# Splitting the last 512 columns of a residual stage, and the first pair of an activation, in a two-block transformer kernel

## The reference, cut to what matters

```python
for i in range(DEPTH_2):
    mod = (c_act @ mod_w[i] + mod_b[i]).reshape(B, 6, D)[:, :, None, :]
    hin = x * (1.0 + mod[:, 1]) + mod[:, 0]
    y = mla_mixer(hin, ...) if i == 0 else moba_mixer(hin, ...)      # ends in  merge_heads(o) @ w_o
    x = layer_norm(DEEPNORM_ALPHA * x + mod[:, 2] * y, ln_g[i, 0], ln_b[i, 0])
    hin = x * (1.0 + mod[:, 4]) + mod[:, 3]
    y = conv_ffn(hin, ffn_w_in[i], ffn_conv_w[i], ffn_conv_b[i], ffn_w_out[i])   # ends in  (gelu(a) * b) @ w_out
    x = layer_norm(DEEPNORM_ALPHA * x + mod[:, 5] * y, ln_g[i, 1], ln_b[i, 1])
return x
```

## Time and profile before

| | |
|---|---|
| runs of the kernel before | 901.68, 901.88, 904.54 us |
| median | 901.88 us |
| the profiled execution | 900.74 us |
| its span, first to last instruction | 898.9 us |
| TensorE busy (matmuls) | 861.6 us, 96% |
| VectorE busy | 683.7 us, 76% |
| ScalarE busy | 449.3 us, 50% |
| GpSimd busy | 69.0 us, 8% |

### The profile page before, as it was taken

The page is one execution under the profiler, slowest core; times in us unless marked ns, Lnnn a source line. Parts: engine busy times, 40 slices in busy tenths (PEclk is TensorE's granted clock), DMA queues, the critical chain, the costliest instruction groups (busy, mean ns, idle before and its releaser), DMA issues.

```text
span 898.9 us, 14495 instructions
## 1 busy us (share of the span) xinstructions
PE 861.6 (96%) x5768; PEld 755.3 (84%) x5768; DVE 683.7 (76%) x1090; ACT 449.3 (50%) x712; POOL 69.0 (8%) x62
## 2 busy tenths in 40 slices
PE   8999989999999999989999999899999899999996
PEld 8988977677876887789899999679987799999995
DVE  5598799878977997789866856796887876656657
ACT  5464554454556545366545445264553665455450
POOL 1000001000001120001200100110000021001001
PEclk9999999989999999999999999999999999999999
DMA  9855567545965870699866797278716885655601
GB/s 337 298 169 195 193 232 240 184 142 197 340 236 211 279 258 1 245 359 354 314 214 230 266 361 262 80 270 318 242 58 247 304 323 184 203 175 185 191 1 47
DMA packets 57028, 201.00 MB, mean 224 GB/s; under 512 B 6600, under 2 KB 7936, under 8 KB 56960
## 3 DMA queue, kind: packets, MB, share of 16 engines
q1 hardware_dynamic: 55952, 196.89, 62.5%
q0 software_dynamic: 1008, 3.18, 1.1%
HBM read 198.96 MB, written 1.08 MB: 223 GB/s over the span
## 4 chain that ended last, share of the span: by engine, by line
PE 81%; DVE 12%; ACT 3%; issue 3%; POOL 0%; DMA 0%; DVEq 0%; ACTq 0%
PE ps L1160 26%; PE ps L1161 25%; PE ps L1162 25%; DVE R L1471 2%; DVE wsp L1408 2%; PE ps L1173 1%; DVE small L1675 1%; PE ps L1345 1%; PE ps L1376 1%; DVE wk L1446 1%; PE ps L1252 1%; PE ps L1352 1%; PE ps L1337 0%; PE ps L1243 0%; DVE pb L1666 0%
## 5 line engine op out<-in xcount | busy, mean ns | idle before, releaser
L1160 PE MATMUL ps<-XT,wsp 128*128 128x256 f32 x768 | 217.3, 283 | 3.9 <-DVE XT L1453 3.0
L1161 PE MATMUL ps<-XT,wsp 128*128 128x256 f32 x768 | 214.5, 279 | 0.0
L1162 PE MATMUL ps<-XT,wsp 128*128 128x256 f32 x768 | 214.2, 279 | 0.0
L1408 DVE TENSOR_TENSOR wsp<-ring,wsp 128x1024 fp32r<-128x1024 f32 x144 | 178.1, 1244 | 9.3 <-ACT wsp L1954 9.3
L1954 ACT CAST wsp<-ring 128x1024 fp32r<-128x1024 f32 x143 | 148.6, 1044 | 61.7 <-PE ps L1162 54.9
L1160 PEld LDWEIGHTS ps<-XT,wsp 128*128 128x128 f32 x768 | 144.0, 187 | 8.4 <-issue 3.9
L1161 PEld LDWEIGHTS ps<-XT,wsp 128*128 128x128 f32 x768 | 144.0, 187 | 0.9
L1162 PEld LDWEIGHTS ps<-XT,wsp 128*128 128x128 f32 x768 | 143.7, 187 | 0.0
L1160 PE MATMUL ps<-wsp,ra 128*128 128x512 f32 x236 | 94.6, 401 | 4.0 <-issue 1.5
L1162 PE MATMUL ps<-wsp,ra 128*128 128x512 f32 x236 | 93.6, 397 | 0.0
L1161 PE MATMUL ps<-wsp,ra 128*128 128x512 f32 x236 | 93.1, 394 | 0.0
(11 more groups left out here) (269 smaller groups left out, 1530.7 us busy)
## 6 DMA issues: line engine op xcount, KB each, us to landing
arena<-in_mod_w SPq DMA_DIRECT2D x50, 512.0 KB, 6.0
ring<-in_mod_w SPq DMA_DIRECT2D x42, 512.0 KB, 4.9
ring<-in_ffn_a SPq DMA_DIRECT2D x28, 512.0 KB, 4.9
ring<-in_ffn_b SPq DMA_DIRECT2D x28, 512.0 KB, 5.2
arena<-in_ffn_o SPq DMA_DIRECT2D x22, 512.0 KB, 4.6
ring<-in_ffn_o SPq DMA_DIRECT2D x22, 512.0 KB, 4.8
arena<-in_ffn_a SPq DMA_DIRECT2D x16, 512.0 KB, 5.9
arena<-in_ffn_b SPq DMA_DIRECT2D x16, 512.0 KB, 4.6
```

The source lines that it names most:

```text
L1160: pe.matmul(o, l[0], r[0], start=start, stop=False)
L1161: pe.matmul(o, l[0], r[1], start=False, stop=False)
L1162: return pe.matmul(o, l[1], r[0], start=False, stop=stop)
L1408: ve.tensor_tensor(w[:, 1024:1024 + n], raw[slot[0]][:, 0:n], w[:, 0:n].bitcast(f32), SUB).then_inc(*done("V", "lo", u, also=[("raw", *slo ...
```

## The change

The last 512 columns of the rows t = 1 are computed as two parts of 256 columns in two banks, q = 2 and q = 3 (column 256 * q on), in both `proj_a` with `halves` and both `ffn`; `resid` is called for each part. The bn_stats of t = 1 are taken over 256 columns always (four groups), those of t = 0 over 512 as before. In `transposed`, the low part of the pair k = 0 is added right behind this pair's conversion instead of behind the next one's, and is done block by block (two subtractions of 256 columns, with two casts of 256); the other pairs stay as they are.

```diff
-            bs = [bank.get(), bank.get()]
+            todo = [(t, c, n, bank.get()) for t, c, n in (
+                ((0, 0, 512), (1, 0, 256), (1, 256, 256)) if halves and cb == blocks - 1 else ((0, 0, 512), (1, 0, 512)))]
...
-                if len(pending) > 1:
+                if len(pending) > 1 or k == 0:
                     low_part()
...
-    def resid(r, i, t, cb, b):
+    def resid(r, i, t, q, n, b):
...
-        if t == 1 and cb == (0 if r else 1) and not final:
+        if t == 1 and q == (0 if r else 2) and not final:
             add("ln_fin", r, i, 0, 512)
...
-        outs = [[bank.get() for _ in range(2)] for _ in range(2)]
+        outs = [(t, q, n, bank.get()) for t, q, n in ((0, 0, 512), (0, 2, 512), (1, 0, 512), (1, 2, 256), (1, 3, 256))]
...
-            for cb in range(2):
+            for part in outs[2:]:
                 for j in js[len(free):]:
-                    piece(1, cb, j)
+                    piece(part, j)
...
+                        if k == 0 and i == 0:
+                            ins.then_inc(*done("V", "xt_f0", tag))
...
+                    if k == 0:
+                        for i in range(2):
+                            for e in new("V", ("xt_hi", tag, 0, i)):
+                                ve.wait_ge(*e)
+                            ve.tensor_tensor(XT[1][i], wk[s[0]][:, i * 256:(i + 1) * 256], XT[0][i].bitcast(f32),
+                                             SUB).then_inc(*done("V", "xt", tag, i, also=[("wk", *s)] if i else []))
+                        continue
...
-                    ve.bn_stats(st[:, (2 * t + cb) * 6:(2 * t + cb) * 6 + 6], X[:, t, cb * 512:(cb + 1) * 512]).then_inc(
-                        *done("V", "res_s", r, i, t, cb))
+                    w = 256 if t else 512
+                    for c in range(q * 256, q * 256 + n, w):
+                        g = c // w * 6
+                        ins = ve.bn_stats(st[t][:, g:g + 6], X[:, t, c:c + w])
+                    ins.then_inc(*done("V", "res_s", r, i, t, q))
```

More of the change, by code:

```diff
@@ L257, in proj_a @@
                 got = [W.next(name, base + cb * nq + q + e) for e in range(m)]
-                for t in range(2):
-                    add("row", x, nk, got, q, t, bs[t], prior("bank", bs[t]), q + m == nq)
+                for t, c, n, b in todo:
+                    add("row", x, nk, got, q, t, b, prior("bank", b), q + m == nq, c, n)
                     if q + m == nq:
-                        evac(t, cb, bs[t])
-                        bank.put(bs[t][0])
+                        if halves:
+                            evac(t, 2 * cb + c // 256, n, b)
+                        else:
+                            evac(t, cb, b)
+                        bank.put(b[0])
                 q += m
@@ L745, in order @@
     final = []
-    def resid(r, i, t, cb, b):
+    def resid(r, i, t, q, n, b):
         W.finish(gn[0])
         until(i, 5 if r else 2)
+        ends = 256 * q + n == 1024
         s = wk.get()
-        add("res_m", r, i, t, cb, b, s, prior("wk", s))
-        if i == 0 and t == 1 and cb == 1:
+        add("res_m", r, i, t, q, n, b, s, prior("wk", s))
+        if i == 0 and t == 1 and ends:
             have.add(("r2", r))
-        if t == 1 and cb == (0 if r else 1) and not final:
+        if t == 1 and q == (0 if r else 2) and not final:
             add("ln_fin", r, i, 0, 512)
-        add("res_a", r, i, t, cb, s)
+        add("res_a", r, i, t, q, n, s)
         wk.put(s[0])
-        add("res_s", r, i, t, cb)
-        if cb:
+        add("res_s", r, i, t, q, n)
+        if ends:
             add("res_z", r, i, t)
@@ L762, in resid @@
                 add("out_g", t, c, final[0])
-        if final and t == 1:
+        if final and t == 1 and (q == 0 or ends):
             for c in range(2):
-                add("out", cb, c, final[1])
+                add("out", int(ends), c, final[1])
     def ffn(i):
-        outs = [[bank.get() for _ in range(2)] for _ in range(2)]
+        outs = [(t, q, n, bank.get()) for t, q, n in ((0, 0, 512), (0, 2, 512), (1, 0, 512), (1, 2, 256), (1, 3, 256))]
         held, hold = [], {}
@@ L774, in second @@
                 w = W.next(f"ffn_o{i}", 2 * u + e)
-                for t in range(2):
-                    for cb in range(2):
-                        o = outs[t][cb]
-                        add("fo", i, u, t, e, cb, w, g, o, prior("bank", o), False, t == 1 and cb == 1)
+                for t, q, n, o in outs:
+                    add("fo", i, u, t, e, q, n, w, g, o, prior("bank", o), False)
                 W.done(w[1])
@@ L1207, in tensor @@
                 elif kind == "row":
-                    x, nk, got, q, t, b, before, full = a
+                    x, nk, got, q, t, b, before, full, c0, n = a
                     tc = slice(t * 128, (t + 1) * 128)
@@ L1839, in vector @@
                 elif kind == "res_a":
-                    r, i, t, cb, s = a
-                    x = X[:, t, cb * 512:(cb + 1) * 512]
-                    tag, n = (("g0", 0), ("g1", 1), ("g2", 1), ("g3", 1))[2 * i + r]
-                    for e in new("V", ("res_m", r, i, t, cb), ("gain", tag, n, t)):
+                    r, i, t, q, n, s = a
+                    x = X[:, t, q * 256:q * 256 + n]
+                    tag, g = (("g0", 0), ("g1", 1), ("g2", 1), ("g3", 1))[2 * i + r]
+                    for e in new("V", ("res_m", r, i, t, q), ("gain", tag, g, t)):
@@ L1991, in scalar @@
                         ins.then_inc(*done("A", "xt_f", tag, k, also=[("bank", *b)]))
+                    for i in range(2 if k == 0 else 0):
+                        for e in new("A", ("xt_f", tag, 0) if i else ("xt_f0", tag)):
+                            ac.wait_ge(*e)
+                        ac.copy(XT[0][i], wk[s[0]][:, i * 256:(i + 1) * 256]).then_inc(*done("A", "xt_hi", tag, 0, i))
+                    if k == 0:
+                        continue
                     for e in new("A", ("xt_f", tag, k)):
```

65 lines of the change are left out of this document (33 added, 32 removed).

## The result

| | before | after |
|---|---|---|
| runs | 9, 900.83 to 904.54 | 9, 905.03 to 908.70 |
| median | 902.31 us | 906.07 us |
| ratio after / before | | 1.0042, 95% interval 1.0028 to 1.0055 |
| the profiled execution (its span) | 900.74 (898.9) | 906.49 (904.7) |

The changed kernel is slower by 3.8 us (interval 2.5 to 5.0). The forecast was +1.9, a median of 903.8, in a range of 901.1 to 906.6. Two executions in this document, one of `after_clock` (1403.75 us, the profiled one) and one of `before_pause` (2152.30 us), are far from all others and stand in no ratio.

The account below looks back on a forecast made before the run. TensorE was taken to bound the kernel (81% of the chain), so only its waits and issue count. Residual ends, pair split and extra matmuls summed to +1.9: 902.65 profiled, median 903.8 us, range 901.1 to 906.6.

Parts of the forecast that it names:

- slower: Outcome that the whole kernel's time lands above the band of no telling change, 899.2 to 904.6 us; chance about 0.31.
- the same: Outcome that the whole kernel's time stays within 0.3% of before, 899.2 to 904.6 us; chance 0.61.
- The residual end: Six short VectorE instructions for three long lengthen the chain TensorE waits for: MLA output +0.75, MoBA output +0.72, first ffn +0.6.
- VectorE is free in time: Rival at the residual ends: the first part's work hides under 1.4 us of matmuls; time 894; 8%, any gain over 0.3% included.
- The pair split: In four activations the first low part comes ahead of the next pair's conversion: two were to gain, two to lose.
- m00 -0.44: Activation after the first block: the first matmul goes earlier, but the third step's weights limit the gain to 0.44 us.
- m10 -0.74: Activation after the first ffn: the first half is low in time, so TensorE's whole wait of 0.74 us goes.
- m01 and m11 +0.31 each: Activations after the MLA and MoBA output projections: matmuls wait for a bank only the sixth conversion frees, 0.31 us lost each.
- with the old bank it would gain up to 0.98: Claim for the activations after the MLA and MoBA output projections: only the bank keeps the split from gaining up to 0.98.
- TensorE (+0.3): In the four split stages, 180 matmuls of 512 columns become 360 of 256; 132 count, at +0.0024 each, +0.3 us.
- The clock: Rival: longer TensorE pauses let its clock fall to half, some 3 us more, 906.8 us; 18%.
- 1.00 around 580: Sign in the profile after: the granted clock stays at its full level around 580 us, near the first ffn's end.

Follow-up runs that it names:

- after_clock: The changed kernel with 14 more transposes, their result overwritten, at the start of TensorE's pause at the first ffn's end; ratio to before 1.0033.
- before_pause: The kernel before with one more unused 512-column bn_stats in VectorE's chain at the first ffn's end, lengthening TensorE's pause; 904.33 us, ratio 1.0020.
- res_join: The changed kernel with one 512-column bn_stats per half of the columns of t = 1 instead of two of 256; 905.70 us, ratio 1.0031.
- the two tail kernels: The kernel before and the changed one, each with t = 0's last two output instructions moved behind the last residual part; run once each, 905.77 and 907.34 us.
- pair_only: The kernel before with only the split of each activation's first pair, residual stages as before; 902.76 us, ratio 0.9997.
- after_bank: The changed kernel with the first ffn product's bank taken ahead of the ffn's five output banks, so one long free; 907.29 us, ratio 1.0048.

## Why the prediction was right, and where it was off

**The side and the range were right**, by the steps given; the size was half of what came. The chance of "slower" was 0.31; most of it was put on "the same", and that was too much, since the sum was 2 short. Of these 1.9, some 0.8 lies in the local terms, which come to 2.7 without a fall of the clock: m01 is 0.4 dearer than forecast, m00 wins 0.2 less, m10 and m11 are 0.1 dearer each. The other 1.1 no run isolates; falls of the clock that come more often can carry it (below). The local terms alone would have given 904.6 to 905; that 906.07 lies inside the range is thanks to the room left in it for the clock, and not to the sum.

**The residual end (+0.75, +0.72, +0.6)**: measured +0.70, +0.69 and +0.55 from behind the last product to the transposes of t = 1. The growth of the waits alone, +0.88 and +0.83, leaves out the earlier start of t = 0's transposes, which the forecast had taken off (at 0.06). The mechanism is the one named: VectorE isn't free when the first part is full. `res_join` and the two tail kernels show both sides of it. From res_a to the aggregate it is 2.23 for the 2.26 of the forecast. Not in the sum was the longer aggregate over four groups, 0.26 for 0.21.

**The rival "VectorE is free in time"** was to decide at over 1.2 us of idle time. With 1.73 it won 0.9, as priced; with 0.42 it won 0.16, and with 0.15 the split lost.

**The pair split**: m00 -0.44, measured -0.33 at the third step (-0.20 in the end), and bounded by this step's weights as said:

```profile
293.02 0.50 PE L1166 MATMUL ps<-wsp,XT 128*128 128x512 f32 x1 [0.36 <-DVE wsp L1415]
```

m10 -0.74: without the clock -0.6 (`pair_only`), in the profile of the changed kernel +0.79 with it. m01 and m11 +0.31 each: measured +0.43 at the eighth matmul and +0.40; TensorE starts 0.15 behind the end of the sixth conversion, where 0.03 was taken. The sentence that with the old bank it would gain up to 0.98 was false: `pair_only` loses 0.30 and 0.21 there with that bank, and `after_bank` shows that no bank would help, because the second pair's low part comes later than before.

**A term left out**: +0.28 in m01 at its fourth product (404.40 before, 407.13 after, where the offset of 2.53 goes to 2.81). VectorE takes a product out of its bank until just before (L1950, from 406.31 for 0.68), so that a wait for this bank is likely; no run isolates it, and the scatter between two profiles is as large in m01.

**TensorE (+0.3)**: the products of ffn 0 alone gave +0.49, those of ffn 1 with their surroundings -0.24; mla_o's -0.17 is the earlier start of t = 0's transposes and nothing of its products. A 256-column step is 0.119 in both ffn after (means), not 0.118, and a 512-column one 0.232 and 0.2335 before. The sum is near the forecast by accident; ffn 1 is faster for its products with `ra` standing, which the change doesn't touch: every 0.1175 in the changed kernel, 0.1187 before. Why is open.

**The clock** was a rival with 18% and 3 us, and the profile after was to show 1.00 around 580; it shows 0.89. The price of a fall is 0.7 to 1.6 here, not 3: the row of 8 us at 0.57 held a longer one (6.8 us, the others 3.4). And a fall behind this pause was not the exception: in seven of ten profiles. The difference between the two profiles holds 0.8 + 0.6 of it in m10. Over many runs: the local terms without a fall sum to 2.7 (4.1 less the 1.4 in m10), the medians differ by 3.8, interval 2.5 to 5.0. The changed kernel's nine runs have a mean clock of 0.9898, the kernel before had 0.9904 to 0.9909 in the sets above, which is 0.3 to 0.6 falls; the other kernels with this pause have 0.8 to 1.1 falls more. At 1.4 each that is 0.4 to 1.5 us, and the 1.1 between lies in it. So falls that come more often, and cost more in m10, can carry the rest; how much each has of it is not shown.

## What to carry to other kernels

Splitting the last part of a chain pays only if the engine behind it is idle when the first part is ready; look for its idle time ahead of that instruction in the timeline, and if there is none, count what the additional instructions cost (here 0.15 each beyond their share of the work, 0.5 to 0.7 in each stage). An operand that is ready earlier is worth only the distance to the next one that isn't, so look at the second wait as well as the first. Where a pool hands out banks in turn, one more that is held shifts every later user, and the new wait shows in the grouped waits under the instruction that frees it. Whether a longer pause costs clock is read from the mean granted clock of many runs; one profile shows only where a fall came in one of them.

## What the runs showed of the hardware

In the thirteen profiles that can be compared the granted clock fell near 180 and 337 us each time, near 120 in eight and near 587 in seven, to 1.2 GHz, for about 3.4 us (0.84 on average over 11 us) or, near 180 in the kernel before, 6.8 us (0.57 over 8 us). With the pause unfilled, whether it fell near 587 went with the fall near 120, 460 us earlier, in ten of ten profiles, and not with the length of the pause in front of it (2.3 with and without a fall, 2.9 with and without). Yet over the runs the mean clock went with the pause: 0.9879 with 2.9 in `before_pause`, 0.9909 with 2.3 in the kernel before, 0.9922 with the pause filled. A fall cost 0.7 to 1.6 us; the median of the kernel before was 902.31 to 903.53 in its four sets of runs. VectorE's instructions of 256 columns took 0.41 to 0.43 for a multiply, an add or a subtraction of two tiles and for bn_stats, against 0.68 to 0.70 of 512; the conversion, a multiply and an add by scalars, took 0.54 for 256.
